# A hybrid mixer and mixture-of-experts layer: a solve with blocks of 32, norms in four rows, VectorE's queue in another order, and expert weights fetched in runs of 32 KB

## The reference

```python
h = rms_norm(x, norm_mix)
proj = h @ w_in                      # g_q g_k g_v g_z, m_q m_k m_v m_o, gates
q, k, v = silu(causal_conv(g_q, g_k, g_v)); q, k = l2_normalize(q), l2_normalize(k)
lower = strict(kb @ k.T * decay)     # kb = k * beta
sol = triangular_solve(lower + eye, [v * beta, kb * exp(gam)])   # gated delta rule
o_a = gated delta rule with sol      # head norm, silu(g_z)
num = p @ v; den = p.sum(-1)         # mLSTM, p = exp(d_log - m) * (q @ k.T)
o_b = num / max(abs(den), exp(-m))   # head norm, sigmoid(m_o)
y = sigmoid(gate_gdn) * (o_a @ w_up_gdn) + sigmoid(gate_ml) * (o_b @ w_up_ml)
x = x + y @ w_out
h = rms_norm(x, norm_ffn)
top 4 of 32 experts by h @ w_router; for each expert and its tokens:
    gu = xb @ w_gate_up[e] + b_gate_up[e]          # 1024 x 2048, gate and up interleaved
    act = gate * sigmoid(1.702 * gate) * (up + 1)  # clamped
    y  += gate_of_token * (act @ w_down[e] + b_down[e])   # 1024 x 1024
out = rms_norm(x + y, norm_final)
```

## Time and profile before

| | |
|---|---|
| median of three runs | 1227.34 us (1226.29 to 1229.55) |
| profiled execution, time / span | 1226.06 / 1223.8 us |
| mean granted TensorE clock | 0.988 |
| busy: PE / PEld / DVE / ACT / POOL | 1158.8 / 598.0 / 310.6 / 128.8 / 21.3 us |
| chain that ended last | PE 62%, DMA 32%, DVE 3% |
| moved by DMA | 443.21 MB, 362 GB/s over the span |

### The profile page before, as it was taken

One profiled execution on the slowest core, in us unless ns is written; L12 is line 12 of the kernel. 1 busy time (PEld: TensorE's weight loads), 2 busy tenths in 40 slices (PEclk: granted clock), 3 DMA queues, 4 the chain that ended last, 5 costly groups with the idle time before them and its releaser, 6 DMA issues.

```text
span 1223.8 us, 13499 instructions
## 1 busy us (share of the span) xinstructions
PE 1158.8 (95%) x5701; PEld 598.0 (49%) x5701; DVE 310.6 (25%) x705; ACT 128.8 (11%) x216; POOL 21.3 (2%) x57
## 2 busy tenths in 40 slices
PE   8989999999999999999989898999999998899996
PEld 7878998876434343433424342434434343334342
DVE  2688432345321120201102020202112020202021
ACT  3551101001000000000000000000000000000001
POOL 1003000000000000000000000000000000000000
PEclk9999999999999999999999999999999999999999
DMA  9944334385999999999999999999999999999994
GB/s 257 383 129 142 111 103 138 110 372 211 381 428 417 428 428 428 428 427 428 427 428 427 428 427 428 427 428 427 427 427 428 428 428 428 428 427 428 428 420 194
DMA packets 63644, 443.21 MB, mean 362 GB/s; under 512 B 8772, under 2 KB 33968, under 8 KB 38016
## 3 DMA queue, kind: packets, MB, share of 16 engines
q1 hardware_dynamic: 57968, 438.38, 86.9%
q10 hardware_dynamic: 4416, 1.99, 0.7%
q0 software_dynamic: 1200, 1.98, 0.5%
HBM read 441.07 MB, written 1.26 MB: 361 GB/s over the span
## 4 chain that ended last, share of the span: by engine, by line
PE 62%; DMA 32%; DVE 3%; SPq 1%; issue 1%; ACT 1%; POOL 0%; ACTq 0%; DVEq 0%
DMA ring<-in_w_down 30%; PE bank L844 22%; PE bank L887 13%; PE bank L549 11%; PE bank L824 3%; PE bank L780 2%; PE bank L926 2%; PE bank L565 1%; SPq L439 1%; PE bank L750 1%; PE bank L739 1%; PE bank L836 1%; DMA ring<-rows_copy 1%; PE bank L901 1%; PE bank L572 1%
## 5 line engine op out<-in xcount | busy, mean ns | idle before, releaser
L844 PE MATMUL bank<-ring,cvg 128*64 128x512 f32 x2112 | 461.9, 593 | 9.5 <-DMA ring<-in_w_gate_up 9.2
L844 PEld LDWEIGHTS bank<-ring,cvg 128*64 128x64 f32 x2112 | 151.3, 137 | 300.8 <-issue 274.5
L887 PE MATMUL bank<-ring,cvg 128*64 128x512 f32 x1024 | 236.5, 618 | 29.4 <-DMA ring<-in_w_down 29.4
L1516 DVE TENSOR_SCALAR cvm<-bank 128x512 f32<-128x512 f32 x33 | 22.8, 692 | 651.0 <-PE bank L844 651.0
L549 PE MATMUL bank<-ring 128*128 128x256 f32 x768 | 169.7, 380 | 4.1 <-DVE cvm L1154 4.1
L887 PEld LDWEIGHTS bank<-ring,cvg 128*64 128x64 f32 x1024 | 80.0, 142 | 183.7 <-issue 183.7
L549 PEld LDWEIGHTS bank<-ring 128*128 128x128 f32 x768 | 144.4, 190 | 23.5 <-ACT ring L1826 3.5
L1896 ACT ACTIVATE cvm<-cvm 128x512 f32<-128x512 f32 x33 | 20.8, 629 | 497.4 <-DVE cvm L1516 497.4
L824 PEld LDWEIGHTS bank<-ltm,hn 128*128 128x128 f32 x544 | 66.6, 196 | 7.3 <-issue 7.1
L824 PE MATMUL bank<-ltm,hn 128*128 128x128 f32 x544 | 66.9, 281 | 0.0
L926 PE MATMUL bank<-vb,ltm 128*128 128x512 f32 x128 | 57.7, 593 | 0.0
(11 more groups left out here) (328 smaller groups left out, 550.8 us busy)
## 6 DMA issues: line engine op xcount, KB each, us to landing
ring<-in_w_gate_up SPq DMA_DIRECT2D x128, 2048.0 KB, 31.5
ring<-in_w_down SPq DMA_DIRECT2D x58, 2048.0 KB, 35.0
ring<-in_w_in SPq DMA_DIRECT2D x24, 1024.0 KB, 6.7
ring<-in_w_down SPq DMA_DIRECT2D x12, 1024.0 KB, 34.0
ring<-in_w_out SPq DMA_DIRECT2D x4, 1024.0 KB, 4.9
ring<-in_w_up_ml SPq DMA_DIRECT2D x2, 1024.0 KB, 5.1
ring<-in_w_up_gdn SPq DMA_DIRECT2D x2, 1024.0 KB, 5.0
xs<-in_x SPq DMA_DIRECT2D x2, 512.0 KB, 4.4
```

The lines of the kernel that those rows point to most:

```text
L844: mm = pe.matmul(B[4 + half][side * SLOTS:(side + 1) * SLOTS, :], xT[:, k, e * SLOTS:(e + 1) * SLOTS], w[:, (k % 2) * PIECE + at:(k % 2) * ...
L887: mm = pe.matmul(B[6 + half][e * SLOTS:(e + 1) * SLOTS, :], actT[:, e, at:at + SLOTS], by_block(double(of[e]), 4)[:, j, half * HALF:(half ...
L1516: dve.tensor_scalar(g2, both[:, :, :, 0], SWIGLU_LIMIT, None, ALU.min).then_inc(sem("glu_g_ready"), 1)
```

## The change

It has two halves, made together.

*Mixer.* The blocks of the solve become 32 x 32 (32 of them, 31 steps), so that one level of the old kind is left, and the last level (blocks of 64 to 128) works on the one quadrant that it changes, 64 x 64 a head and tile. The solve's steps stand in VectorE's queue in two parts. The norms are summed into four rows, one a head, by products with columns of `select`; root and reciprocal run on 4 x 256, and the rows go through DRAM to all partitions, on POOL's queue. The gate scalars are computed token by token, without a copy and a second turn. The mLSTM v gets a column of ones, so that num and den come from one product of 129 columns; the fourth head's go to bank 4, and so does the turned k. The bias's work on VectorE stands behind vb. The second tile's router work is divided, and the counts (L954 to L960) move into gate_up(0, 0). The two early expert fetches come later.

*Experts.* Rows are dealt to partitions in runs of 4 (gate_up) and 8 (down), 32 KB. Two doubles in adjacent places come in one fetch of 4 MB, a quad, which waits until both are free; the first ten doubles come singly, in 16 KB runs, and the last six in halves. hn is written in the order in which gather wants it, and gate_up reads columns as 8 of every 16.

```diff
-        doubles.extend((DN, col, side) for side in range(2) for col in weights_of(g))
+        doubles.extend((DN, col, side) for col in weights_of(g) for side in range(2))
...
-        ring_order = [4, 3, 5, 8, 6, 7, 1, 2, 0, 9]
+        ring_order = [4, 5, 6, 7, 8, 9, 2, 3, 0, 1]
+        fill_order = [4, 3, 5, 8, 6, 7, 1, 2, 0, 9]
...
-        BASE = 16
+        BASE = 32
         NB = P // BASE
-        LEVELS = [16, 32, 64]
+        LEVELS = [32]
...
-        base_in = mixer_only(BASE * BASE)[0:NB * H * T, :].rearrange("q (p f) -> q p f", p=BASE)
-        base_out = mixer_only(2 * BASE * BASE)[0:NB * H * T, :].rearrange("q (i r c) -> q i r c", i=2, r=BASE)
+        base_out = hn[0:NB * H * T, :, :].rearrange("q i (r c) -> q i r c", r=BASE)
...
+        norm_copy = nc.dram_tensor("norm_copy", [2, H, S], F32).ap()
...
+        quads_released = [d for d in released if d[2] % 2 == 1]
+
+        def place_free(i):
+
+            was = quads_released[i // 2 - DOUBLES // 2]
+            return release_of[was] + 1
...
+            s = ring_order[i] if i < DOUBLES else place_at[quads_released[i // 2 - DOUBLES // 2]] - 1 + i % 2
+            place_at[d] = s
+            whole = i >= DOUBLES and d not in HALVED
+            if whole and i % 2 == 1:
+                s -= 1
+            else:
+                turns[s] += 1
+            turn_at[d] = s, turns[s] - 1
...
-        gu_v = w_gate_up.rearrange("l e (i p j) c -> (l e) p i (j c)", p=P, j=2)
-        dn_v = w_down.rearrange("l e (m p j) c -> (l e) p m (j c)", p=P, j=4)
+        gu_v = w_gate_up.rearrange("l e (q p j) c -> (l e) p q (j c)", p=P, j=4)
+        dn_v = w_down.rearrange("l e (q p j) c -> (l e) p q (j c)", p=P, j=8)
...
+            def fetch_quad(i, e):
+                kind, col, part = doubles[i]
+                src = (gu_v, dn_v)[kind][bass.ds(e, 1), :, part // 2, :].rearrange("e p c -> p e c")
+                s = place_at[doubles[i]]
+                dst = ring[:, s:s + 2, :].rearrange("p a c -> p (a c)")
+                sp.dma_start(by_block(dst, 1), src).then_inc(sem(full(s)[0]), 16)
...
-                if j in (RING, RING + 2):
-                    fetch((j - RING) // 2, fixed(0))
...
+                if j in (RING + 12, RING + 14):
+                    i = ring_order.index(fill_order[(j - RING - 12) // 2])
+                    fetch(i, fixed(doubles[i][1]))
...
-            for i in range(DOUBLES, len(doubles) - len(HALVED)):
+            for i in range(DOUBLES, len(doubles) - len(HALVED), 2):
...
-                sp.wait_ge(sem("double_done"), i - DOUBLES + 1)
-                fetch(i, expert[col])
+                sp.wait_ge(sem("double_done"), place_free(i))
+                fetch_quad(i, expert[col])
...
-            for pair in (HALVED[0:2], HALVED[2:4], HALVED[4:5], HALVED[5:6]):
-                sp.wait_ge(sem("double_done"), doubles.index(pair[-1]) - DOUBLES + 1)
+            for pair in ((HALVED[0], HALVED[2]), (HALVED[1], HALVED[3]), HALVED[4:5], HALVED[5:6]):
+                sp.wait_ge(sem("double_done"), max(place_free(doubles.index(d)) for d in pair))
...
+            def keep_norms(n):
+                pool.wait_ge(sem("rows_ready"), n + 2)
+                pool.dma_start(norm_copy[n], norms[:, n, :]).then_inc(sem("norms_kept"), 16)
+
...
+            keep_norms(0)
             pool.wait_ge(sem("rows_kept"), 32)
             pool.dma_start(spread_rows, rows_copy.partition_broadcast(P)).then_inc(sem("rows_spread"), 16)
+            spread_norm(0)
+            keep_norms(1)
             pool.dma_start(spread_runmax, runmax_copy.partition_broadcast(P)).then_inc(sem("runmax_spread"), 16)
+            spread_norm(1)
...
-            pe.wait_ge(sem("hT_ready"), 2 * T)
-            for k in range(KC):
...
-            mm.then_inc(sem("scal_rows_done"), 1)
...
-            for t in range(T):
-                mm = pe.transpose(B[5][:, t * 4 * H:(t + 1) * 4 * H], scal_rows[:, t * P:(t + 1) * P], ident[0:4 * H, 0:4 * H])
+            for t in range(T):
+                pe.wait_ge(sem("hT_ready"), 2 * t + 2)
+                for k in range(KC):
+                    mm = pe.matmul(B[5][:, t * 4 * H:(t + 1) * 4 * H], hT[:, k, t * P:(t + 1) * P], wsc[:, k, :],
+                                   start=(k == 0), stop=(k == KC - 1))
...
+            def norm_sums(n):
+                for h in range(H):
+                    mm = pe.matmul(B[2][0:H, n * S:(n + 1) * S], select[:, H - 1 - h:2 * H - 1 - h], attn[:, h, :, :],
+                                   start=(h == 0), stop=(h == H - 1))
+                mm.then_inc(sem("norm_sums"), 1)
...
                 per_head((4, 5), "q_done", lambda h, t: (t1[:, h, t, :], invT[:, h, t, :]))
+
+            def last_t1():
+
+                pe.wait_ge(sem("inv_ready"), len(LEVELS))
+                for i in range(H * T):
+                    h, t = i // T, i % T
+                    mm = pe.matmul(B[0][UPPER, i * HP:(i + 1) * HP], lt[LOWER, h, t, UPPER], inv[LOWER, h, t, LOWER],
+                                   start=True, stop=True)
+                mm.then_inc(sem("t1_done"), 1)
+
+            def last_q():
+
+                pe.wait_ge(sem("t1_ready"), len(LEVELS) + 1)
+                for i in range(H * T):
+                    h, t = i // T, i % T
+                    mm = pe.matmul(B[4][LOWER, i * HP:(i + 1) * HP], t1[UPPER, h, t, LOWER], invT[UPPER, h, t, UPPER],
+                                   start=True, stop=True)
+                mm.then_inc(sem("q_done"), 1)
 
...
             pe.wait_ge(sem("proj_taken"), 2)
             pe.wait_ge(sem("pt_ready"), H)
+            pe.wait_ge(sem("kd_ready"), 1)
             for t in range(T):
...
-                        mm = pe.matmul(B[4][:, t * H + h:t * H + h + 1], pt[:, h, t + j, :], ones[:, 0:1],
-                                       start=(j == 0), stop=(j == t))
+                        dst = B[2 + t][:, h * (DH + 1):(h + 1) * (DH + 1)] if h < H - 1 else B[4][:, t * (DH + 1):(t + 1) * (DH + 1)]
+                        mm = pe.matmul(dst, pt[:, h, t + j, :], mv_s[:, j, h, :], start=(j == 0), stop=(j == t))
...
             pe.wait_ge(sem("base_loaded"), 16 + 16 * 2 * NB)
             level_t1(0)
-            proj(15)
-            pe.wait_ge(sem("ml_sums_taken"), 1)
+            proj(17)
             level_pq(0)
-            proj(16)
...
+            for n in range(2):
+                for i in out_bank(0, n):
+                    pass
+            for i in out_bank(1, 0):
+                if i == 0:
+                    turn_x2(0, 0)
+                    turn_x2(0, 1)
+                if i == 2:
+                    router(0, 0)
+                    router(0, 1)
+            for i in out_bank(1, 1):
+                if i == 0:
+                    turn_x2(1, 0)
+                if i == 1:
+                    pe.wait_ge(sem("chosen_ready"), 1)
+                    pe.matmul(ranks[0], striu[:, :], chosen[:, 0, :], start=True, stop=True).then_inc(sem("ranks_done"), 1)
+                if i == 2:
+                    router(1, 0)
+            turn_x2(1, 1)
...
-                        by_row = hn[:, t, :].rearrange("s (i p j) -> s i j p", p=P, j=2)
-                        mm = pe.matmul(B[6 + b][:, (k % 4) * P:(k % 4 + 1) * P], by_row[:, k // 2, k % 2, :],
+                        mm = pe.matmul(B[6 + b][:, (k % 4) * P:(k % 4 + 1) * P], hn[:, t, k * P:(k + 1) * P],
                                        onehot[:, t, :], start=(t == 0), stop=(t == T - 1))
                 mm.then_inc(sem("gathered"), 1)
...
+            def columns(w, half, side):
+
+                return w.rearrange("p (h f s c) -> p h s f c", h=2, s=2, c=8)[:, half, side, :, :]
...
-                        at = side * FE + half * HALF
                         mm = pe.matmul(B[4 + half][side * SLOTS:(side + 1) * SLOTS, :], xT[:, k, e * SLOTS:(e + 1) * SLOTS],
-                                       w[:, (k % 2) * PIECE + at:(k % 2) * PIECE + at + HALF], start=False,
+                                       columns(w[:, (k % 2) * PIECE:(k % 2 + 1) * PIECE], half, side), start=False,
...
+            def count_items():
+
+                pe.wait_ge(sem("gates_ready"), 1)
+                for t in range(T):
...
+                    if n == 0 and e == 0 and i == 0:
+                        count_items()
...
-                dve.wait_ge(sem("roots_ready"), root)
-                r = t1[:, :, :, :].rearrange("p h t i -> p h (t i)")
-                link(dve.reciprocal(r, r))
+            def invert_norms(n):
+                dve.wait_ge(sem("roots_ready"), n + 1)
+                dve.reciprocal(norms[:, n, :], norms[:, n, :]).then_inc(sem("rows_ready"), 1)
+
+            def normed(n, first, const, done):
+                dve.wait_ge(sem("norms_spread"), 16 * (n + 1))
...
-                for j in range(BASE - 1):
+
+            def solve_base(first, end):
+
+                for j in range(first, end):
...
                     link(dve.tensor_tensor(v, v, step, ALU.subtract))
```

(31 more changed lines are left out.)

255 lines of the change are left out of this document (121 added, 134 removed).

## The result

Seven runs of each kernel: 1236.41 us median (1236.12 to 1239.78) against 1227.72 (1225.96 to 1232.77). The ratio is 1.0069, 95% interval 1.0051 to 1.0086: the change is **slower by 0.7%, some 8.5 us**, where 1226.9 and no difference were forecast.

The account below looks back on a forecast made before the run. TensorE bounds until gate_up, then the DMA engines fetching expert weights. Terms -4.1 (steps 1 to 3), +10.2 idle and -6.5 rate sum to -0.4 us against the profiled execution, giving 1226.9 us, range 1217 to 1236.

Parts of the forecast that it names:

- Step 1: Mixer up to the mLSTM sums: -0.7 us; lt ready at 80.7, kd0 at 132.3, TensorE waiting some 8 us.
- Rival (a): Faster: second norm lands when asked for, VectorE 3 us earlier to kd0, clock stays up; 1218.4 us, chance 0.32.
- (d): Slower: VectorE's queue before kd0 later still because the base blocks come late; +5 us gives 1232, chance 0.08.
- Step 2: From the mLSTM sums to gate_up: -8.2 us, including +2.0 for a lower clock; gate_up at 295.0.
- Step 3: First expert fetch: +4.8 us, as the DMA engines restart 8.2 us after gate_up starts instead of 3.4.
- Step 4: Idle DMA engines in the expert stage: +10.2 us, 1.8 at down(0), 6.9 plus 1.5 at SHARED.
- Step 5: Rate of expert weight fetches: -6.5 us, 32 KB runs moving 430.7 to 431.6 GB/s instead of 428.
- Rival (b): Slower: 32 KB runs move expert weights no faster while step 4's idle stays; 1233.4 us, chance 0.17.
- Step 6: Elsewhere nothing: gate_up's 2% slower operand reads hide in TensorE's waits; last six doubles and tail as before.
- Rival (c): Slower: TensorE becomes the bound through gate_up's broken-up moving operand; 1325 us at 1.5 times, chance 0.03.

Follow-up runs that it names:

- Run 5: The changed kernel with its first six quads fetched as two doubles, each waiting for its own place only: 1238.49 us, ratio 1.0081 to the kernel before.
- run 4: The changed kernel with each quad fetched in two 2 MB transfers of 16 KB runs, issued when both places are free: 1233.37 us, ratio 1.0034 to before.
- Run 8: The changed kernel with only the last two w_down quads before the halves fetched as four doubles, order first, third, second, fourth: 1233.13 us, ratio 1.0035 to before.

## Why the prediction was wrong

It forecast -0.4 us on the profiled span and got +10.9. By its own steps:

- **Step 1, up to the sums: the place where it failed first.** The wait came as described: 7.42 us for "some 8", released by kd0, the queue from lt to kd0 51.4 us for 51.6 worked out (84.23 to 135.62), with solve steps of 0.41 us at 252 elements (L1336) where the formula gives 0.41. But lt was ready at 84.23, not 80.7. The windows up to it, before:

```profile
0.00:89.07 89.07, 79.69 (x400) 68.33 (x401) 50.99 (x97) 44.47 (x69) 6.87 (x31) 1.00 0.81 256
```

and after:

```profile
0.00:84.23 84.23, 80.80 (x414) 69.60 (x415) 40.89 (x99) 41.92 (x66) 8.04 (x29) 0.98 0.79 235
```

VectorE's work fell by 10.1 us, not 12.0, and its idle time rose from 38.1 to 43.3, 5.3 us where 3.6 were allowed. The chain shows the second norm's way:

```profile
61.52 2.16 DMA norm_copy<-vb
...
63.97 5.82 DMA ring<-norm_copy
```

From the end of its root's reciprocal (61.25) to the landing (69.79) are 8.5 us: two transfers one behind the other, while the step took half of one transfer's 9.8. A part is not the kernel's but the execution's: in the eleven other profiles with this mixer lt ended between 81.35 and 84.25, after's is at the late end. The median of all twelve is 83.1, so some 2.4 us of the 3.5 are the kernel's. gate_up starts between 295.9 and 301.2 in the eight of them that keep kd0 where it is, never at 295.0. So kd0 came 3.3 us later than forecast and, as VectorE alone sets it, gate_up with it. Rival (a) went the wrong way on this very link, (d) had the right link for another reason (the late norm and not the base blocks, which landed as the queue reached them).
- **Step 2, from the sums to gate_up: right.** Forecast -8.2; 135.76 to 299.06 is 163.3 us against 170.9 before, -7.6. The clock fell for the sums alone (4.80 for 2.68 us), the 2.0 foretold; the 64x64 products took 1.07 us a set for 0.9.
- **Step 3, +4.8 for the first quad: right as a time, wrong as a separate cost.** The first quad was issued 8.5 us behind gate_up, 8.2 forecast. Run 5 shows that undoing it alone brings nothing: the idle moves to the stretch before down(0)'s end.
- **Step 4, +10.2 of idle: the mechanism right at both places, undersized.** 3.5 us for 1.8 near 370, 9.3 for 8.4 near 760. Near 370 down(0) was done 71.1 us behind gate_up's start (299.06 to 370.20), not 67: it took 15.6 us, not 14, and the trace of before shows the same 15.65 at 358.23, ending about 70 us behind gate_up. TensorE's waits for w_down were 0.5 to 7.0 us, at eleven downs, not some 8 at each.
- **Step 5, -6.5 by the rate: right.** 431 GB/s, inside the 430.7 to 431.6 worked out, and run 4, with the quads cut in two, has 427. On the 862 us 0.7% are 6 us. Whether the gain is the longer run's or the larger transfer's no run shows; both halve in number. The Trainium skill's fixed cost for a packet (DMA: Bandwidth & Descriptors, Why small descriptors are slow) would make it an estimated 2.5 us, and these windows show more than twice that. Rival (b) is out.
- **Step 6, "the tail is as before": wrong, +4.6 us.** This term was missing. The hand-written sequence tracked the DMA engines; it wrote down that a down starts only with both quads, and did not follow that to the last downs, where no further transfer hides it. The timelines show where it comes from. Before waits for the two sides of its last full down apart:

```profile
1130.11 8.78 PE L887 MATMUL bank<-ring,cvg 128*64 128x512 f32 x32 [2.42 <-DMA ring<-in_w_down]
...
1139.90 7.09 PE L887 MATMUL bank<-ring,cvg 128*64 128x512 f32 x32 [1.01 <-DMA ring<-in_w_down]
```

When the pair's last double has landed, half a down is left, and the end is 83.9 us away (1139.90 to 1223.8). After, with the quad landed, the whole down is left, 16.55 us for 7.09, of which 2.6 are the lower clock (13.95 at the full one), and the end is 89.9 us away (1144.78 to 1234.7). Of these 9.5 us 3.4 come back, mostly the 2.6 us that before still waits for weights behind this point and after does not. So 6.0 us more of TensorE's way stand on a landing that is 4.9 us later: 10.9, the whole difference in span. The end is no longer the last transfer and 25 us, as the prediction's first paragraph has it, but TensorE's own work from 1144.78 on. Run 8 takes the wait for the quad away and gets 1 to 4 us back, until the DMA engines bind again.
- **Rival (c), the broken-up columns:** gate_up's 64 matmuls take 13.73 us as in the earlier trace rows. It costs nothing.

4.0 at gate_up, 2.6 of idle and 4.6 of tail are 11.2 of the 11.3 us between forecast and result; the rate has the other 0.1. The largest is the tail, which step 6 put at nothing. All three lie on one side, and part of the first is this execution's. The range, which ends at 1236, held each slow case alone and left pairs of misses out, and it was a sum of three that came, none of them large.

## What to carry to other kernels

A larger transfer is, in this ring, one event for three parties: it waits for all of its places, lands whole, and gives its places back late. Price those first at the points without slack (the start, a step whose buffers are held longer, the last consumers), and only then the gain in rate; there split it, and keep the large form where there is slack. And when a wait is moved to an earlier point in one engine's queue, look at what stands ahead of its releaser in the other's: here a step without a deadline stood ahead of kd0, and putting it behind was worth more than the whole first half of the change.
